# Projecting the last tile ahead of five normalisations in two parts of its tokens

## What is computed

```python
def _rms(x, g):
    xf = x.astype(jnp.float32)
    y = xf * lax.rsqrt(jnp.mean(xf * xf, axis=-1, keepdims=True) + EPS)
    return y.astype(x.dtype) * g
...
# first block, each of two layers
hx = _modulate(_rms(x, norm_mix_g[i]), sx1, cx1)
x = x + gx1 * (mixer(hx) @ w_out)          # conv/Fourier mixer, then neighbourhood attention
x = x + gx2 * _mlp(_modulate(_rms(x, norm_mlp_g[i]), sx2, cx2), mlp_w1[i], mlp_w2[i])
...
# second block, each of two layers
y = mixer(rms_norm(h, pre_norm), w_in, w_out)   # sliding window + conv, then stick breaking
h = h + rms_norm(y, post_norm)
```

## Time and profile before

| | us |
|---|---|
| median of 3 runs | 2262.72 |
| lowest and highest of the 3 | 2261.09, 2267.88 |
| the profiled execution's own time | 2260.53 |
| its span | 2258.7 |
| PE busy in the span | 2127.0 (94%) |
| DVE, ACT, POOL busy | 1231.8, 796.2, 675.9 |

### The profile page before, as it was taken

The page is one execution under the profiler, slowest core; times in us unless marked ns, Lnnn a source line. Parts: engine busy times, 40 slices in busy tenths (PEclk is TensorE's granted clock), DMA queues, the critical chain, the costliest instruction groups (busy, mean ns, idle before and its releaser), DMA issues.

```text
span 2258.7 us, 33098 instructions
## 1 busy us (share of the span) xinstructions
PE 2127.0 (94%) x13426; PEld 1828.8 (81%) x13426; DVE 1231.8 (55%) x1617; ACT 796.2 (35%) x1292; POOL 675.9 (30%) x314
## 2 busy tenths in 40 slices
PE   5998989999999998998999999999999896999987
PEld 3888878888888886898777888888898685988866
DVE  5885777544465546671954322223789425067752
ACT  4213232212122215443863333223333633255542
POOL 1332223222222222322983444444031224300002
PEclk9999999999999999999999999999998897999998
DMA  8343415233242321232222333333222010221111
GB/s 305 135 147 120 150 32 179 89 98 116 84 154 97 121 58 47 74 71 61 32 56 75 108 89 95 99 93 94 71 81 65 11 57 29 84 66 57 57 47 38
DMA packets 74954, 199.93 MB, mean 89 GB/s; under 512 B 25296, under 2 KB 26576, under 8 KB 74832
## 3 DMA queue, kind: packets, MB, share of 16 engines
q1 hardware_dynamic: 73648, 197.60, 28.6%
q10 hardware_dynamic: 1184, 0.61, 0.1%
HBM read 194.51 MB, written 2.10 MB: 87 GB/s over the span
## 4 chain that ended last, share of the span: by engine, by line
PE 83%; DVE 7%; POOL 4%; ACT 2%; issue 2%; DMA 1%; SPq 0%; DVEq 0%; ACTq 0%
PE ps L2108 59%; PE ps L2228 6%; PE ps L2595 5%; PE ps L2123 3%; POOL NAP L883 2%; PE ps L2644 1%; DVE ada_acc L1435 1%; DMA ADA<-stream 1%; PE ps L2619 1%; PE ps L2631 1%; PE ps L2291 1%; PE ps L2148 1%; DVE UC L1815 1%; DVE S L1731 1%; POOL S L853 1%
## 5 line engine op out<-in xcount | busy, mean ns | idle before, releaser
L836 POOL TENSOR_TENSOR WL<-raw,WH 128x1024 fp32r<-128x1024 f32 x215 | 524.2, 2441 | 1289.4 <-ACT WH L933 1289.3
L933 ACT ACTIVATE WH<-raw 128x1024 fp32r<-128x1024 f32 x260 | 274.0, 1056 | 487.7 <-PE ps L2108 458.9
L2108 PE MATMUL ps<-HH,WH 128*128 128x512 f32 (+2 forms) x1560 | 416.8, 333 | 4.2 <-DVE HL L1917 2.5
L2108 PE MATMUL ps<-HL,WH 128*128 128x512 f32 (+2 forms) x1560 | 415.7, 333 | 0.0
L2108 PE MATMUL ps<-HH,WL 128*128 128x512 f32 (+2 forms) x1560 | 413.8, 332 | 0.0
L2108 PEld LDWEIGHTS ps<-HH,WH 128*128 128x128 f32 x1560 | 250.0, 188 | 39.0 <-DVE HL L1917 2.7
L2108 PEld LDWEIGHTS ps<-HH,WL 128*128 128x128 f32 x1560 | 249.8, 188 | 31.2
L2108 PEld LDWEIGHTS ps<-HL,WH 128*128 128x128 f32 x1560 | 249.8, 188 | 30.6
L2108 PE MATMUL ps<-GH,WH 128*128 128x512 f32 (+1 forms) x896 | 266.2, 355 | 3.0 <-issue 3.0
L2108 PE MATMUL ps<-GL,WH 128*128 128x512 f32 (+1 forms) x896 | 266.3, 355 | 0.0
L2108 PE MATMUL ps<-GH,WL 128*128 128x512 f32 (+1 forms) x896 | 264.3, 352 | 0.0
(11 more groups left out here) (279 smaller groups left out, 3399.6 us busy)
## 6 DMA issues: line engine op xcount, KB each, us to landing
raw<-stream SPq DMA_DIRECT2D x260, 512.0 KB, 3.6
ring<-stream SPq DMA_DIRECT2D x80, 512.0 KB, 3.8
ADA<-stream SPq DMA_DIRECT2D x4, 2048.0 KB, 19.2
XT<-rpb SPq DMA_DIRECT2D x128, 24.0 KB, 2.4
XT<-xT SPq DMA_DIRECT2D x1, 2048.0 KB, 8.6
out<-XT SPq DMA_DIRECT2D x8, 256.0 KB, 2.0
V1s<-V SPq DMA_DIRECT2D x6, 256.0 KB, 4.7
XT<-ctxT SPq DMA_DIRECT2D x1, 1024.0 KB, 11.1
```

Source lines behind the costliest of these rows:

```text
L836: nc.gpsimd.tensor_tensor(WL[:, slot, :], raw[:, slot, :], WH[:, slot, :].bitcast(F32), ALU.subtract).then_inc(lo_done[slot], 1)
L933: nc.scalar.activation(WH[:, slot, :], raw[:, slot, :], ACT.Copy).then_inc(hi_done[slot], 1)
L2108: ins = nc.tensor.matmul(pair(g)[:, cols], lhs, x[:, k, cols], start=first, stop=last)
```

## The change

The last tile of `out1`, of the last `down` chunk of both layers, of `out3` and of `out4` is no longer one run over the inner dimension with both column slices in each step. It becomes two runs: first all matmuls of the first `CUT` tokens, then all matmuls of the rest. `out2` is left as it was. A new semaphore `half_full` is raised behind the first run, and the update (or copy), the square and the sum are made for each part by itself: `half_x`, `half_sq` and `half_sum` count those of the first part. PE waits for `half_sum` ahead of the means of the first part's tokens and for the whole sum ahead of the first token tile that the rest touches. Where 512 tokens lay in one bank (`down1`, `out4`), the rest is written at column 512, the pair's second bank (`REST_AT`).

The cuts: 512 of 768 for `out1` and `down0`, 256 of 512 for `down1` (the norm behind it has 528 tokens, so its rest is 272), 264 of 528 for `out3`, 256 of 512 for `out4`.

```diff
+        CUT = {"out1": NX, "down0": NX, "down1": NX // 2, "out3": N2 // 2, "out4": NX // 2}
+        REST_AT = {"out1": NX, "down0": NX, "down1": NX, "out3": N2 // 2, "out4": NX}
+        NORM_LAST = {1: "out1", 2: "down0", 4: "down1"}
...
 # ACT, square
+                if j == KT_D - 1 and r in NORM_LAST:
+                    first = CUT[NORM_LAST[r]]
+                    act.wait_ge(half_x, HALF_AT[NORM_LAST[r]])
+                    nc.scalar.activation(dst[:, 0:first], XT[:, j, 0:first], ACT.Square).then_inc(half_sq, 1)
+                wait_x(act, r, j)
+                nc.scalar.activation(dst[:, first:n], XT[:, j, first:n], ACT.Square).then_inc(sq_done, 1)
...
 # ACT, post
+                    if m == KT_D - 1:
+                        first = CUT[kind]
+                        act.wait_ge(half_full, HALF_AT[kind])
+                        nc.scalar.activation(y[:, m, 0:first], pair(g)[:, 0:first], ACT.Copy).then_inc(half_x, 1)
+                        act.wait_ge(half_x, HALF_AT[kind])
+                        nc.scalar.activation(dst[:, 0:first], y[:, m, 0:first], ACT.Square).then_inc(half_sq, 1)
+                    full(g)
+                    at = first and REST_AT[kind]
+                    nc.scalar.activation(y[:, m, first:n], pair(g)[:, at:at + n - first], ACT.Copy).then_inc(ps_free[g % 4], 1)
...
 # DVE, mixer_out (out1)
+                        norm_sum(r, m - 1)
+                        half_x_update(g, kind, layer, 2)
+                        half_norm_sum(r)
+                        rest_x_update(g, m, layer, 2, kind, n)
+                        products_beside((kind, m))
+                        norm_sum(r, m, CUT[kind])
+                        return
...
 # DVE, mlp_down (down0, down1)
+                        norm_sum(r, m - 1)
+                        half_x_update(g, kind, layer, 5)
+                        rest_x_update(g, m, layer, 5, kind, MLP_N[layer])
+                        half_norm_sum(r)
+                        norm_sum(r, m, CUT[kind])
+                        return
...
 # PE, project
+                for some in [column_parts(n)] if cut is None else [[slice(0, CUT[cut])], [slice(CUT[cut], n)]]:
+                    for k in range(depth):
...
+                    if cut is not None and some[0].start == 0:
+                        ins.then_inc(half_full, 1)
...
 # PE, norm (and the same in post)
+                def summed(t):
+                    if r in NORM_LAST:
+                        if t == 0:
+                            pe.wait_ge(half_sum, HALF_AT[NORM_LAST[r]])
+                        if t != CUT[NORM_LAST[r]] // P:
+                            return
+                    pe.wait_ge(sq_used, 7 * (r - 1) + 7)
```

More of the change, by code:

```diff
@@ L569, in build @@
         sq_used = sem("sq_used")
+        half_full = sem("half_full")
+        half_x = sem("half_x")
+        half_sq = sem("half_sq")
+        half_sum = sem("half_sum")
         rstd_done = sem("rstd_done")
@@ L1495, in first_cols, with norm_sum @@
                 dve.wait_ge(amul_done, i + 1)
-            def norm_sum(r, j):
+            def norm_sum(r, j, first=0):
                 n = NORM_N[r]
@@ L1953, in post @@
                 for m in range(1, KT_D):
-                    dve.wait_ge(y_sq, KT_D * layer + m + 1)
+                    first = 0
                     if m >= 2:
                         dve.wait_ge(y_sq_used, 7 * layer + m - 1)
-                    nc.vector.tensor_tensor(S2[:, 0:n], S2[:, 0:n], (S0, S1)[m % 2][:, 0:n], ALU.add).then_inc(y_sq_used, 1)
+                    if m == KT_D - 1:
+                        kind = ("out3", "out4")[layer]
+                        first = CUT[kind]
+                        dve.wait_ge(half_sq, HALF_AT[kind])
+                        nc.vector.tensor_tensor(S2[:, 0:first], S2[:, 0:first], S1[:, 0:first], ALU.add).then_inc(half_sum, 1)
+                    dve.wait_ge(y_sq, KT_D * layer + m + 1)
+                    nc.vector.tensor_tensor(S2[:, first:n], S2[:, first:n], (S0, S1)[m % 2][:, first:n], ALU.add)\
+                      .then_inc(y_sq_used, 1)
                 rstd(GROUP["postc", layer], n, post_rstd)
@@ L2095, in column_parts, with project @@
                 return (slice(0, NX), slice(NX, n)) if n > NX else (slice(0, n),)
-            def project(g, tile, h, n, depth=KT_D, width=P, col=0, ready=None, q=None, st=0, sg=0):
+            def project(g, tile, h, n, depth=KT_D, width=P, col=0, ready=None, q=None, st=0, sg=0, cut=None):
                 weights(tile, q, st)
                 empty(g, q, sg)
[L2101 to L2108, removed]
+                to = 0 if cut is None else REST_AT[cut] - CUT[cut]
+                for some in [column_parts(n)] if cut is None else [[slice(0, CUT[cut])], [slice(CUT[cut], n)]]:
+                    for k in range(depth):
+                        if ready is not None:
+                            ready(k)
+                        for i, (w, x) in enumerate(parts(tile % 4, h)):
+                            lhs = w[:, k * width + col:k * width + col + P]
+                            first, last = k == 0 and i == 0, k == depth - 1 and i == 2
+                            for cols in some:
+                                at = cols if cut is None or cols.start == 0 else slice(cols.start + to, cols.stop + to)
+                                ins = nc.tensor.matmul(pair(g)[:, at], lhs, x[:, k, cols], start=first, stop=last)
+                    if cut is not None and some[0].start == 0:
+                        ins.then_inc(half_full, 1)
                 ins.then_inc(ps_full[g % 4], 1)
@@ L2304, in _ @@
             for m in range(KT_D):
-                project(GROUP["out1", m], TILE["out1", m], (GH1, GL1), N1, ready=mixed if m == 0 else None)
+                project(GROUP["out1", m], TILE["out1", m], (GH1, GL1), N1, ready=mixed if m == 0 else None, cut="out1" if m == KT_D - 1 else None)
                 if m == 5:
```

57 lines of the change are left out of this document (38 added, 19 removed).

## The result

The changed kernel takes 2252.76 us (median of 5 runs, 2250.32 to 2255.88); the ratio to the kernel before is 0.9948, with a 95% interval from 0.9933 to 0.9962. In a second set of runs, with runs of the kernel before beside them, it was 2253.76 and 0.9951 (0.9934 to 0.9968); one of the six executions of that set took 5292.44 us, was in the slow state and is left out of the ratio. By these ratios that is 11 to 12 us less, beyond the 0.3% that I called distinguishable. The forecast was 2253.4 with a range from 2248.5 to 2259.5.

What follows compares the result with a forecast made beforehand. PE's work was taken as the bound, its waits before norm means as winnable. Five places gave 8.0 us, the clock 1.3, together 9.3 off a median of 2262.72: 2253.4, range 2248.5 to 2259.5.

Steps and rivals of the forecast that it cites:

- What bounds it, and the prices: Whole kernel: PE is 83% of the chain; winnable are its waits before norm means, with squares, sums and updates priced from rows.
- the signs: Profile after: PE idle near 0 then 0.4 us in `out1`, 1.1 in `down0`; 0.7 or so in `out3` and `out4`.
- The fixed 0.15 us: Each added instruction costs about 0.15 us of fixed time, counted in the sum where it lies on the path.
- `out1`, `down0`, `out3`, `out4`: Last tiles of these stages: means or root come earlier, gains of 3.3, 2.0, 1.2 and 1.35 us.
- the table load would be late next: `out3` and `out4`: the root's 1.28 us table load stands behind the last square; without it `out4` gains 1.7, not 1.35.
- `down1`: Layer 1's last down tile: DVE is late by a sum under a POOL instruction; gain 0.2 us, or 1.3 if not late.
- The clock: Spreadings behind `out1` and `down0`: one half on average escapes the half clock, 1.3 us, bounds 0 and 2.6.
- in `out3` and `out4` I count nothing: Spreadings there: the clock falls about when the spreading starts in both versions, so no clock gain is counted.
- Rival (a): Clock stays up through all spreadings and into first projections: 9 us at most, about 5 likely; time 2249; chance 0.12.
- (b): DVE or ACT late in more places, or longer hops, and no clock gain: gain 4 to 6.5 us, about 2257.5; chance 0.26.
- (c): Split tiles: weight loads come into the open, 0.071 us for each of 156 matmuls, 11 us; time 2265.8; chance 0.04.
- (d): Nothing changes, as the means wait for something the trace blames wrongly; time 2262.7; chance 0.02.

Runs made afterwards that it cites:

- pool_waits: Changed kernel, with POOL's subtraction for the third tile of `in3` waiting until the sums of layer 1's last down tile are done; 2251.50 us, ratio 0.9944.
- before_fill_sums: Kernel before, with idle matmuls of 128 columns in PE's wait for the sums at the five places, no work moved; 2258.44 us, ratio 0.9975.
- before: The kernel before the change, unaltered; median 2265.81 us in the largest set, of 35 runs.

## Why the prediction was right, point by point

**What bounds it, and the prices.** The reading of the waits held at all five places, and so did the durations: 0.63 and 0.42 for the squares, 0.69 and 0.43 for the sums, as the rows of other lines had said. The waits left to PE came out longer than the signs said, 0.70 us in `out1` for 0.4, 1.27 in `down0` for 1.1 and 1.06 in `out3` for 0.7. The fixed 0.15 us of each added instruction was only paid where it lay on the path, and there it was in the sum. The Trainium skill, VectorE: DVE Perf Modes, section on the TRN2 errata, advises tiles of at least 512 elements; here cuts below that paid.

**`out1`, `down0`, `out3`, `out4`.** 3.1, 1.9, 1.15 and 1.3 us against 3.3, 2.0, 1.2 and 1.35. Each is a little short; in `out1` it is because the last four records of means took 0.61, not 0.50. Outside these stretches the split tile itself takes longer on PE, from its first matmul to its last by 0.08 us in `out1`, 0.03 in `down0`, 0.07 in `down1`, nothing in `out3` and 0.16 in `out4`, where the 256-column matmuls have a pitch of 0.120 us, not 0.117. That the table load would be late next was right, and that it would cost little too.

**`down1`.** Right, with its reason: DVE was late by a sum that lay under POOL's subtraction, which `pool_waits` showed by removing it, with a gain of 1.0 us in the trace (the estimate had been 1.3).

**The clock.** This is the term that was mis-sized. The mechanism was the forecast one, the size 1.3 against 3 in the two profiles. The step that fell short is "in `out3` and `out4` I count nothing" together with taking half for the two spreadings. In the profile after, `down0`'s spreading ran at full clock and `out1`'s for the most part (1.57 and 1.90 against 2.9), 2.3 us in place of 1.3; `out4`'s ran at full (1.13 for eight records against 2.04) and `out3`'s in part (2.21 against 2.58), 1.3 us in place of nothing. That the clock falls about when the spreading starts in both versions was wrong for `out4`: before, it had fallen amid the means already (1.37 us for eight records that take 1.05 at full in `before_fill_sums`), and after, it fell behind the spreading, so there was more to win than the prediction saw. Rival (a), in which it all comes back (9 us), did not happen: in the profile after the clock is still at half behind `out1`, `down0`, `out2` and `down1`. The idle matmuls behind the spreadings then took another 5 to 6 us off by the times.

**The rivals.** (b) did not happen: no piece was late but the one in `down1`, and the clock gave more, not nothing. (c) was ruled out by the run made for it and by the pitch in `out4`, where 24 loads came on top. Its count of 156 matmuls was too high from the start: the page before has a weight load for every matmul, so of the 156 only 36 bring a new one, 2.6 us at its own price. (d) was ruled out by the result.

**The base.** The forecast was given from a median of three runs that was 3 us lower than those of the larger sets. I should have said that three runs between 2261.09 and 2267.88 leave the base itself open by some 3 us.

## What to carry to other kernels

Where a reduction over everything stands between two dense stages, cut the last producer tile by the dimension that the reduction does not cross: the epilogue of the first part is hidden, and what remains is the epilogue of the smaller part, if every engine on the chain is on time. Look at the engine queue ahead of the split point first; one blocked instruction there takes the whole gain, as in `down1`. And price a short wait of TensorE at more than its length: at the five places before, waits of 12.8 us cost some 5.6 more by the clock, and a few matmuls in the wait, into columns that nobody reads, got that back. Compare medians of many executions for this, not two profiles.

## What the runs showed of the hardware

- TensorE's granted clock fell to half (1.2 GHz) behind waits of 2.1 to 3.2 us followed by the single-column matmuls of the means (`before`), and in `out1` of the changed kernel also behind waits of 0.70 and 0.67 us around them. It fell at other points of the same code in another execution: in one profile the spreading in `down0` took 1.57 us, in another 2.90. The time of the whole kernel spread over 7.9 us in the kernel before (2260.89 to 2268.77 in 23 runs), over 4.2 with idle matmuls in the waits for the sums (2256.42 to 2260.64 in 12), and over 13.1 with idle matmuls behind the spreadings (2254.23 to 2267.31 in 12).
- Idle matmuls alone, without any work moved, made the kernel before 0.25% faster (2258.44 against 2264.03); the five spreadings behind them took 7.5 us in place of 12.1.
- A weight load of 0.188 us per matmul stayed hidden under 256 columns: the pitch was 0.120 us in `out4` and 0.117 in the window of the earlier trace rows. The record counts show one load for every matmul also where two in a row use the same weight (13426 and 13426). An `out1` tile in two runs took 8.47 us against 8.40; what the small differences come from isn't shown.
- A sum on VectorE with both inputs in SBUF took 2.48 us under GpSimd's subtraction and 0.71 when the subtraction was moved (`pool_waits`).
